# Two transformer blocks on one core: squares of the first norm, casts of the gate stages and activation table loads put in another order

## The reference, cut to what matters

```
def rms_norm(x, gain):
    xf = x.astype(jnp.float32)
    y = xf * lax.rsqrt(jnp.mean(xf * xf, axis=-1, keepdims=True) + NORM_EPS)
    return (y * gain.astype(jnp.float32)).astype(x.dtype)

for l in range(DEPTH):            # DEPTH = 2
    x = x + 0.5 * rms_norm(swiglu(rms_norm(x, ln_ffn1_pre[l]), w_ffn1_in[l], w_ffn1_out[l]), ln_ffn1_post[l])
    mix = token_mixing(rms_norm(x, ln_mix_pre[l]), ...)     # window attention, mLSTM, RWKV-7
    x = x + rms_norm(mix, ln_mix_post[l])
    x = x + 0.5 * rms_norm(swiglu(rms_norm(x, ln_ffn2_pre[l]), w_ffn2_in[l], w_ffn2_out[l]), ln_ffn2_post[l])
    gate = jax.nn.sigmoid(rms_norm(x, ln_ple_pre[l]) @ w_ple_gate[l])
    x = x + rms_norm(gate * (p[l] @ w_ple_proj[l]), ln_ple_post[l])
```

## Time and profile before

| | us |
|---|---|
| median of 3 runs | 2913.27 |
| lowest, highest | 2912.16, 2914.24 |
| the profiled execution | 2914.65 |
| its span | 2912.9 |
| TensorE busy | 2849.4 (98%) |
| VectorE busy | 1380.4 (47%) |
| ScalarE busy | 1139.1 (39%) |

### The profile page before, as it was taken

How to read it: one execution, slowest core, us unless ns; L and a number is a source line. 1 busy time by engine, 2 the same in 40 slices (tenths; PEclk the granted TensorE clock), 3 DMA queues, 4 the chain that set the end, 5 groups by cost and what they waited for, 6 DMA issues and landing times. The chain is left out here.

```text
span 2912.9 us, 41085 instructions
## 1 busy us (share of the span) xinstructions
PE 2849.4 (98%) x17248; PEld 2402.7 (82%) x17248; DVE 1380.4 (47%) x1923; ACT 1139.1 (39%) x1635; POOL 15.7 (1%) x29
## 2 busy tenths in 40 slices
PE   7999999999999999999999999999999999999998
PEld 7888888778888888888888877888888889888887
DVE  3333355676333355333336667333346268755641
ACT  3223244545222245222234545332236357534430
POOL 0000000000000000000000000000000000000000
PEclk9999999999999999999999999999999999999999
DMA  4223412103223431223412103122432111222231
GB/s 146 100 94 127 146 35 66 42 3 116 80 95 103 143 122 46 94 94 102 157 51 71 58 8 110 57 96 95 137 123 95 51 56 33 102 73 94 99 126 51
DMA packets 71558, 254.48 MB, mean 87 GB/s; under 512 B 8072, under 2 KB 9224, under 8 KB 71376
## 3 DMA queue, kind: packets, MB, share of 16 engines
q1 hardware_dynamic: 71376, 251.86, 25.8%
HBM read 249.73 MB, written 2.10 MB: 86 GB/s over the span
## 5 line engine op out<-in xcount | busy, mean ns | idle before, releaser
L214 PE MATMUL ps<-h_hi,w_space 128*128 128x512 f32 (+1 forms) x5056 | 1445.4, 369 | 3.4 <-DVE h_lo L312 3.4
L214 PEld LDWEIGHTS ps<-h_hi,w_space 128*128 128x128 f32 x5056 | 919.4, 189 | 164.1 <-DVE h_lo L312 4.2
L202 DVE TENSOR_TENSOR w_space<-w_raw,w_space 128x1024 fp32r<-128x1024 f32 x440 | 533.5, 1224 | 1014.2 <-ACT w_space L195 1014.1
L214 PE MATMUL ps<-h_lo,w_space 128*128 128x512 f32 (+1 forms) x2528 | 930.3, 368 | 0.0
L195 ACT CAST w_space<-w_raw 128x1024 fp32r<-128x1024 f32 x440 | 455.5, 1047 | 898.1 <-PE ps L214 551.0
L224 PE MATMUL ps<-w_space 128*128 128x512 f32 x3216 | 737.3, 390 | 1.3 <-PEq L91 0.8
L224 PEld LDWEIGHTS ps<-w_space 128*128 128x128 f32 x3216 | 601.8, 188 | 126.1 <-issue 1.2
L214 PEld LDWEIGHTS ps<-h_lo,w_space 128*128 128x128 f32 x2528 | 478.0, 189 | 77.9 <-issue 0.5
L589 ACT CAST w_space<-act_p 128x512 fp32r<-128x512 f32 x88 | 54.7, 621 | 186.2 <-DVE act_p L601 186.2
L604 DVE TENSOR_TENSOR w_space<-act_p,w_space 128x512 fp32r<-128x512 f32 x88 | 60.9, 692 | 60.5 <-ACT w_space L589 60.5
L601 DVE TENSOR_TENSOR act_p<-act_s,ps 128x512 f32<-128x512 f32 x88 | 59.9, 681 | 54.9 <-PE ps L214 54.9
(11 more groups left out here) (415 smaller groups left out, 2191.8 us busy)
## 6 DMA issues: line engine op xcount, KB each, us to landing
w_raw<-in_w_ffn_in SPq DMA_DIRECT2D x176, 512.0 KB, 3.4
w_raw<-in_w_ffn_out SPq DMA_DIRECT2D x88, 512.0 KB, 3.5
w_raw<-in_w_in SPq DMA_DIRECT2D x64, 512.0 KB, 3.5
w_raw<-in_w_up SPq DMA_DIRECT2D x44, 512.0 KB, 3.4
w_raw<-in_w_out SPq DMA_DIRECT2D x24, 512.0 KB, 4.0
w_raw<-in_w_down SPq DMA_DIRECT2D x22, 512.0 KB, 3.5
w_raw<-in_w_ple_gate SPq DMA_DIRECT2D x16, 512.0 KB, 3.5
gain_pre<-in_gains_pre SPq DMA_DIRECT2D x10, 512.0 KB, 4.9
```

Source lines behind the costliest of these rows:

```text
L202: nc.vector.tensor_tensor(self.lo(n), self.raw[:, n % SLOTS, :], self.hi(n).bitcast(F32), ALU.subtract).then_inc(self.lo_ready, 1)
L214: m = nc.tensor.matmul(c.ps[:, bank, t], part[:, cols], moving[:, k, t], start=(k == 0 and i == 0), stop=(k == KD - 1 and i == 2))
```

## The change

Three edits. In `Start`, ACT squares tiles 0 and 1 before its first casts, and DVE's list follows. In `Ple`, the casts for the following product move behind h_hi (two in tile 1, two in tile 2, two after tile 3), and the sums of rest follow. A new helper `table` issues a root or exponent of one element into a tile that nothing reads, so that the table of that function is loaded there: ahead of the first square, after each sigmoid of the gate stage, and in the recurrence after `steps_of_state` and after `squares`. On TensorE, SP and GpSimd no instruction is moved.

```
+def table(nc, c, function):
+    nc.scalar.activation(c.unread[:, c.tables:c.tables + 1], c.eps[:, 0:1], function)
+    c.tables += 1
...
 # class Start, scalar
         act.wait_ge(self.c.made, 4)
-        for n in range(NT):
-            self.turn.scalar_pre(act, nc, n)
-            if n:
-                self.turn.scalar_hi(act, nc, n - 1)
-            self.c.W.hi_to(act, nc, n + 1)
-        self.turn.scalar_hi(act, nc, NT - 1)
-        self.c.W.hi_to(act, nc, EARLY)
+        table(nc, self.c, ACT.Sqrt)
+        turn.scalar_pre(act, nc, 0)
+        turn.scalar_pre(act, nc, 1)
+        for n in range(2):
+            turn.scalar_hi(act, nc, n)
+            W.hi_to(act, nc, n + 1)
+        for n in range(2, NT):
+            turn.scalar_pre(act, nc, n)
+            W.hi_to(act, nc, n + 1)
+        for n in range(2, NT):
+            turn.scalar_hi(act, nc, n)
+        W.hi_to(act, nc, EARLY)
...
 # class Start, vector
+        turn.vector_pre(dve, nc, 0)
+        turn.vector_pre(dve, nc, 1)
+        turn.vector_lo(dve, nc, 0)
+        W.lo_to(dve, nc, 1)
+        turn.vector_lo(dve, nc, 1)
+        W.lo_to(dve, nc, 2)
+        turn.vector_pre(dve, nc, 2)
+        W.lo_to(dve, nc, NT)
+        turn.vector_pre(dve, nc, 3)
...
 # class Ple, scalar
             nc.scalar.activation(c.s_wide, pair(c, self.gate_bank(n)),
                                  ACT.Sigmoid).then_inc(c.sigmoid, 1)
+            table(nc, c, ACT.Sqrt)
             if n:
                 self.turn.scalar_hi(act, nc, n - 1)
+            if 0 < n < NT - 1:
+                c.W.hi_to(act, nc, self.end() + 2 * n)
             act.wait_ge(c.gated, self.l0 + n + 1)
             self.turn.scalar_post(act, nc, n, c.p_wide)
             self.turn.scalar_pre(act, nc, n)
-            if n == 0:
-                c.W.hi_to(act, nc, self.end() + 2)
-            if n == 2:
-                c.W.hi_to(act, nc, self.end() + EARLY)
         self.turn.scalar_hi(act, nc, NT - 1)
+        c.W.hi_to(act, nc, self.end() + EARLY)
 # class Ple, vector
             if n:
                 self.turn.vector_lo(dve, nc, n - 1)
+            if 0 < n < NT - 1:
+                c.W.lo_to(dve, nc, self.end() + 2 * n)
             dve.wait_ge(c.sigmoid, self.l0 + n + 1)
...
-            if n == 0:
-                c.W.lo_to(dve, nc, self.end() + 2)
-            if n == 2:
-                c.W.lo_to(dve, nc, self.end() + EARLY)
         self.turn.vector_lo(dve, nc, NT - 1)
+        c.W.lo_to(dve, nc, self.end() + EARLY)
...
 # recurrence, scalar
                     powers(t, 1)
                     if t:
                         steps_of_state(t - 1)
+                        table(nc, c, ACT.Exp)
                     powers(t, 2)
...
                     if t:
                         squares(t - 1)
+                        table(nc, c, ACT.Sqrt)
                     solution(t)
```

More of the change, by code:

```diff
@@ L465, in scalar @@
     def scalar(self, act, nc):
+        turn, W = self.turn, self.c.W
         act.wait_ge(self.c.made, 4)
-        for n in range(NT):
-            self.turn.scalar_pre(act, nc, n)
-            if n:
-                self.turn.scalar_hi(act, nc, n - 1)
-            self.c.W.hi_to(act, nc, n + 1)
-        self.turn.scalar_hi(act, nc, NT - 1)
-        self.c.W.hi_to(act, nc, EARLY)
-    def vector(self, dve, nc):
[L476 to L482, removed]
+        table(nc, self.c, ACT.Sqrt)
[10 more added lines that the diff above has]
+        W.hi_to(act, nc, EARLY)
+    def vector(self, dve, nc):
+        turn, W = self.turn, self.c.W
+        turn.vector_pre(dve, nc, 0)
[7 more added lines that the diff above has]
+        turn.vector_pre(dve, nc, 3)
+        turn.vector_lo(dve, nc, 2)
+        turn.vector_lo(dve, nc, 3)
+        W.lo_to(dve, nc, EARLY)
     def scalar_tables(self, act, nc):
@@ L3319, in place @@
     c.eps, c.half_pi, c.freq = sb("eps", [P, 3]), sb("half_pi", [P, 1]), sb("freq", [P, 1])
-    c.first_root = sb("first_root", [P, 1])
+    c.first_root, c.unread = sb("first_root", [P, 1]), sb("unread", [P, 32])
+    c.tables = 0
     c.rope = sb("rope", [P, 2, S])
```

## The result

| | before | changed |
|---|---|---|
| median, us (9 runs each) | 2912.61 | 2925.57 |
| lowest, highest | 2911.45, 2919.11 | 2919.22, 2930.99 |
| profiled execution | 2914.65 | 2925.57 |
| its span | 2912.9 | 2923.8 |

The ratio is 1.0041 (95% interval 1.0031 to 1.005): slower, by 13 us. The prediction had 2924.4.

A forecast was written before the change was run, and what follows sets the result against it. TensorE, busy 2849.4 of 2912.9 us, was taken to bound the kernel. Span 2912.9 - 2.1 (start) - 0.5 (recurrences) + 11.1 (gate stages) + 2.6 (clock) = 2924.0; against the median, 2913.27 + 11.1 = 2924.4, range 2917 to 2929.

The forecast's parts named there:

- The start: Before the first product: tiles 0 and 1 squared first, root's table loaded early; first product at 17.1, not 19.18, 2.1 us less.
- some 13 us: At the start: the most the edits could remove of TensorE's idle stretches of 11.0, 1.38 and 2.89 us.
- The recurrence: Two recurrences, table loads moved: between +0.5 and -0.7 us each, -0.25 taken, -0.5 for both.
- Both its signs: Recurrence: `rec_x` 0.44 us late three times, against waits of 1.33 at t = 2 and hardly 0.2 at t = 3 gone.
- The gate stage's lists: Each gate stage: ACT waits at the fourth cast, TensorE then waits 5.35 us at tile 2; stage 5.55 longer, 11.1 for both.
- The clock: TensorE's clock after the new gate-stage wait: 0 to 2.6 us per stage, 1.3 taken, 2.6 for both.
- falls in full: Rival for both gate stages: the clock falls in full, 2.6 us each, 2927.0 in all; chance 0.22.
- The places are free: Rival for the gate stages: the casts' wait is hidden, a stage costs 0.8 us, 2912.3, no change; chance 0.13.
- The faster case: Rival: places free and load done before h_hi is due; each gate stage's three waits go, 3.24 us twice, 2904.2; chance 0.05.

The follow-up runs named there:

- the changed kernel once more: The changed kernel, unaltered, run again for a second profile: 2927.18 us.
- the filled kernel: The whole change plus 24 matmuls on TensorE, results overwritten, ahead of the transposes of tile 2 in each gate stage: 2924.24 us, ratio 1.0033.
- the kernel with one cast ahead: The changed kernel, but in the gate stages the fourth cast goes back behind tile 2's norms, the third stays ahead: 2918.2 us, ratio 1.0019.
- that with none: The changed kernel, but both casts of tile 2 in the gate stages stand behind its norms as before: 2912.25 us, ratio 0.9998.

## Why the prediction was right

**The start** was put at −2.1 and gave −2.55. The mechanism is as told; x tile 1 landed by 9.18 rather than at the 9.5 worked out from its issue and landing time, and h_lo started at 15.35, not 15.8. The size differs between executions, as the other profiles show. With the new order the first product starts at 16.4 to 16.6 in five profiles, and at 17.3 to 17.4 in three, where x tile 1 landed near 9.9 (the changed kernel once more is one of them). The old order has 19.1 to 19.3 in five. Also, that the change to the higher level moved with the work, as I took it, holds for the pair of profiles and is no rule: by the durations it came 3.8 to 6.2 us behind the first product, in executions of either order. At 30 us, kernels with the old start are up to 1.1 us ahead of the profile before, for that reason alone. The eight profiles with the new order are 2.68 ahead there on average, the five with the old one 0.49, which leaves 2.2 for the change. (The cap of "some 13 us" in the prediction should be 15.3, the sum of 11.0, 1.38 and 2.89; nothing hangs on it.)

**The recurrence** was put at −0.25 each. The first gave −0.46: −0.71 by the tables and +0.2 by a longer wait for a transfer of selectors ahead of them. The second moved by −2.54 with what surrounds it, of which the tables have the same −0.7. The rest is not of the lists: TensorE's wait for that transfer, 1.47, was gone (in part because the matmuls ahead of it ran in a low stretch of 6.8 us that was 3.4 before), and the low stretch of the profile before at 1738 was absent. The term was too small because each late `rec_x` cost 0.3, not 0.44. Both its signs are shown: with the root's table `rec_x` is later (0.34), and without it the exponent's gives 1.40 (I had 1.53).

**The gate stage's lists** were put at +5.55 each, and the filled kernel measures 5.4 and 5.75. By steps, after subtracting the 3.01 by which the stage was entered early: gate product 3 at 1121.4 (predicted 1121.7), `act_p` 8.5 late (8.6), transposes of tile 2 at 1137.8 (1137.95), wait 5.22 (5.35). The chain from `act_p` to `h_tokens` took 6.99, reckoned as 7.01. One sum of the working is off: from root 2 at 1135.95, load, sigmoid, load and one-element root come to 1139.7, not 1140.0. By that the old wait at tile 3 would be just used up and the stage 5.35 longer. In the filled kernel 0.12 to 0.16 of the wait is left. Two small misses of reading: the wait for h_lo in tile 1 shrank by 0.37, not 0.5, and both casts waited, while I had thought of the fourth alone as binding. The fourth is the binding one, since with it behind the norms 4.1 of the 5.22 are gone. But the third costs too: the kernel with one cast ahead has stages 2.25 longer, that with none 0.55. The third waits 3.06 for TensorE there too, so most of its price is the wait for its place and not its 2 us of work.

**The clock** was the term with no row: 0 to 2.6 per stage, 1.3 taken. It was 1.5, 2.4, 2.35 and 1.3 in the four stages measured, 1.9 on average. It fell in all eight waits of 5.2 to 5.6 us, so the rival "falls in full" had the event right. Its 2.6 was reached in none. Part of each low stretch lay inside the wait, where it costs nothing: 3.9, 5.7, 5.7 and 3.3 of the 6.8 us lay behind it. The 1.3 that I took, for which no row spoke, is the lowest of the four. The Trainium skill, TensorE: Matmul & The Clock Gate, section Part 1: The HAM clock gate, has it that idle time brings the half rate; the eight low and four filled stages agree. The falls in the recurrences came without such a wait.

**Sum.** Stage by stage, +6.91 and +8.10 stand against 6.85 predicted for each. The total came within 1.2 us, 2925.6 against 2924.4, by terms that were too small in both directions: more gained at the start, more lost to the clock. Two parts of the profile's difference had no term at all, −1.8 in the second recurrence and +1.46 in the second block (a low stretch of 3.4 us at 2388), and they nearly cancel. With nine runs from 2919.2 to 2931.0, that the median is so near is partly luck; the wait and its path are not.

**The rivals.** "The places are free" fell at the first L195 of tile 2, which waits 3.06 for TensorE. The faster case fell with it, though most of its idea holds once the load stands behind h_hi: that kernel takes 2902.3. That the rival had 2904.2 is chance, since its places were free and no cast went back behind the norms.

**The table load.** In the changed kernel too it takes 1.28 and ends with the next instruction 0.01 to 0.02 behind, and it starts 0.02 behind the sigmoid (1113.65 and 1.03 long), so the drain that the Trainium skill, ScalarE: Activation LUTs, section What ACT_TABLE_LOAD costs, adds to a switch appears nowhere here: in all 13 profiles each load starts within 0.02 of the end of the instruction before it.

**What stays open.** Why the other runs of the filled kernel (2922.8 to 2924.9) lie above its two profiled ones (2917.1, 2918.2): by its median, filling the wait gained only 1.3 us over the changed kernel (ratios 1.0033 and 1.0041, with intervals that overlap). So it is shown for the gate stages of two executions, and not for the kernel's time, that filling the wait saves the price of the clock. Also open is why the kernel with one cast ahead loses more to the clock than that with none. Low stretches of 3.4 to 10.2 us come in 12 of the 13 profiles at the start of the recurrences (near 562 and 1680) or at the end of the second one (1738 to 1772), where TensorE's waits are short but many, and in three profiles in the attention of the second block (2380 to 2388). They differ from one execution of a kernel to the next: in two profiles of the changed kernel the second recurrence had 6.8 at 1681 in one, 3.4 at 1683 and 10.2 at 1772 in the other. What sets them was not tried.

## What to carry to other kernels

Before moving an instruction that reuses a slot, look up who held the slot last and when that one is done: on an in-order engine its wait is paid by everything queued behind it, here a norm, for which TensorE then waited 5.2 us. "Idle time" for a table load is the stretch in which nothing behind it is wanted. Behind the sigmoid, ahead of h_hi, it made a gate stage 2.9 longer; behind h_hi it is part of a kernel whose stages are 2.6 shorter. And a new wait of TensorE can cost more than its length: here 5.2 to 5.6 us of it brought another 1.3 to 2.4. Last, one profile per kernel can mislead by a microsecond or more wherever the clock differs between executions. The distance between two matmuls of one stage repeated to 0.03 us in stages left alone, and is the better measure.

## What the runs showed of the hardware

- A wait of 5.2 to 5.6 us in an otherwise busy stretch brought TensorE to its lower level (1.2 instead of 2.4 GHz) in 8 of 8 cases. The clock began to fall before the wait ended and was low for 6.8 us; eight transposes took 1.97 instead of 1.04. Waits up to 2.4 us in the gate stages left it high but for one short stretch.
- In the recurrences, with no wait above 1.5 us there, the clock was low for 3.4 to 10.2 us at a time in 12 of 13 profiles, also of the kernel before. Executions of one kernel differ with their mean clock: with one cast ahead, 2912.97 at 0.998 and 2925.85 at 0.993.
- At the start TensorE came to its higher level 3.8 to 6.2 us behind its first product, by the durations of its matmuls, and differently in executions whose start has the same lists. The record of the granted clock reads 1.00 all through it.
- A table load took 1.28 us in all 13 profiles, and started within 0.02 us of the end of the instruction ahead of it. Ahead of a cast that TensorE needed, the load and its one-element root made TensorE's wait 1.2 to 1.5 us longer.
